# Attention units of a hybrid encoder layer in another order, and stream outputs copied in two steps

## The reference

```python
def block(i):                       # prompt, queries of 128-row block i
    s = jnp.where(mask, _mla_logits(qb, k_nope, kpe), NEG_INF)
    p = jax.nn.softmax(s, axis=-1)
    return jnp.einsum('bhqk,bkhd->bqhd', p, v)
# streams, branch A: softmax over 128 cached + 16 new latent keys
p = jax.nn.softmax(_mla_logits(q, k_nope, kpe_all), axis=-1)
# streams, branch B: the same keys, with a sink in the denominator
e = jnp.exp(s - m); p = e / (jnp.sum(e) + jnp.exp(sink - m))
o = jnp.einsum('bgjtk,bkgd->btgjd', p, v_all)
proj = jnp.einsum('btnc,ncd->btnd', stack([o_mla, o_swa]), w_branch)
```

## Time and profile before

| | |
|---|---|
| median of 3 runs | 882.08 us (881.89 to 882.47) |
| the profiled execution, its own time | 882.5 us |
| its span (first to last instruction) | 880.7 us |
| TensorE busy, share of the span | 861.0 us, 98% |
| VectorE busy | 565.5 us, 64% |
| ScalarE busy | 401.7 us, 46% |
| granted TensorE clock | 1.0 in the whole span |

### The profile page before, as it was taken

The page is one execution under the profiler, slowest core; times in us unless marked ns, Lnnn a source line. Parts: engine busy times, 40 slices in busy tenths (PEclk is TensorE's granted clock), DMA queues, the critical chain, the costliest instruction groups (busy, mean ns, idle before and its releaser), DMA issues.

```text
span 880.7 us, 13801 instructions
## 1 busy us (share of the span) xinstructions
PE 861.0 (98%) x5347; PEld 779.8 (89%) x5347; DVE 565.5 (64%) x930; ACT 401.7 (46%) x813; POOL 36.6 (4%) x56
## 2 busy tenths in 40 slices
PE   8999999999999989999999999999999999999997
PEld 7888999998667769998799999999999998888886
DVE  5548799948845775654789777777777774433224
ACT  5213464436545664434765545445444552333112
POOL 0300000060510000000000000000000000000000
PEclk9999999999999999999999999999999999999999
DMA  7513253569340004538331332223322335222203
GB/s 278 166 45 93 53 155 116 150 194 212 58 119 1 1 2 146 179 109 311 104 109 49 97 96 84 72 85 97 96 75 73 95 120 214 78 90 73 72 24 120
DMA packets 117969, 94.87 MB, mean 108 GB/s; under 512 B 25376, under 2 KB 101168, under 8 KB 117760
## 3 DMA queue, kind: packets, MB, share of 16 engines
q1 hardware_dynamic: 115744, 90.12, 33.9%
q0 software_dynamic: 896, 1.92, 0.7%
q10 hardware_dynamic: 1264, 1.94, 0.6%
HBM read 81.83 MB, written 12.40 MB: 107 GB/s over the span
## 4 chain that ended last, share of the span: by engine, by line
PE 86%; DVE 6%; ACT 5%; issue 1%; DMA 1%; DVEq 0%; POOL 0%; ACTq 0%; POOLq 0%
PE ps L1350 25%; PE ps L1351 25%; PE ps L1352 25%; PE ps L1551 2%; PE ps L1562 1%; PE ps L1600 1%; DMA raw<-in_w_out 1%; PE ps L1524 1%; PE ps L1405 1%; PE ps L1594 1%; ACT probs L1062 1%; PE ps L1646 1%; DVE sc_lo L2366 1%; DVE nm_c L2071 1%; DVE x_t L1872 1%
## 5 line engine op out<-in xcount | busy, mean ns | idle before, releaser
L1859 DVE TENSOR_TENSOR wlo<-raw,whi 128x1024 fp32r<-128x1024 f32 x43 | 52.4, 1223 | 117.1 <-ACT whi L929 109.6
L929 ACT ACTIVATE whi<-raw 128x1024 fp32r<-128x1024 f32 x43 | 45.3, 1059 | 162.6 <-PE ps L1352 160.6
L1206 ACT ACTIVATE t_hi<-wd 128x512 fp32r<-128x512 f32 x84 | 52.8, 628 | 60.2 <-DVE wd L2345 55.8
L1350 PE MATMUL ps<-sc_hi,t_lo 128*128 128x320 f32 x252 | 77.9, 309 | 1.0 <-DVE t_lo L2291 1.0
L1351 PE MATMUL ps<-sc_lo,t_hi 128*128 128x320 f32 x252 | 77.8, 309 | 0.0
L1352 PE MATMUL ps<-sc_hi,t_hi 128*128 128x320 f32 x252 | 77.8, 309 | 0.0
L1350 PE MATMUL ps<-whi,gu_lo 128*128 128x512 f32 x190 | 74.0, 390 | 0.2 <-DVE gu_lo L2415 0.2
L1352 PE MATMUL ps<-whi,gu_hi 128*128 128x512 f32 x190 | 73.9, 389 | 0.0
L1351 PE MATMUL ps<-wlo,gu_hi 128*128 128x512 f32 x190 | 73.9, 389 | 0.0
L2291 DVE TENSOR_TENSOR t_lo<-wd,t_hi 128x512 fp32r<-128x512 f32 x84 | 57.5, 685 | 2.0
L1351 PE MATMUL ps<-h_lo,b_hi 128*128 128x320 f32 x168 | 51.8, 308 | 0.0
(11 more groups left out here) (326 smaller groups left out, 2409.1 us busy)
## 6 DMA issues: line engine op xcount, KB each, us to landing
raw<-in_w_gate_up SPq DMA_DIRECT2D x44, 512.0 KB, 3.8
raw<-in_w_down SPq DMA_DIRECT2D x22, 512.0 KB, 3.6
raw<-in_w_in SPq DMA_DIRECT2D x16, 512.0 KB, 3.9
raw<-in_w_in SPq DMA_DIRECT2D x12, 480.0 KB, 5.1
gates_scratch<-g_out SPq DMA_DIRECT2D x16, 320.0 KB, 2.4
gate_r<-gates_scratch SPq DMA_DIRECT2D x8, 640.0 KB, 4.0
raw<-in_w_branch SPq DMA_DIRECT2D x8, 512.0 KB, 5.5
raw<-in_w_out SPq DMA_DIRECT2D x8, 512.0 KB, 6.3
```

The lines of the kernel that those rows point to most:

```text
L929: act.activation(whi[:, r % 2, :] if to is None else to, raw[:, r, :], ACT.Copy).then_inc(w_hi, 1)
L1206: act.activation(op_parts(kind, p)[0][:], op_source(kind, p), ACT.Copy).then_inc(op_hi_rdy, 1)
L1350: pe.matmul(out, left[1], right[0], start=first, stop=False, skip_group_check=not own_group)
L1859: dve.tensor_tensor(lo[:, place, :], raw[:, r, :], hi[:, place, :].bitcast(F32), ALU.subtract).then_inc(w_lo, 1)
```

## The change

The order of the units changes from unit 8 on. Block 1 (256 wide) is now paired with the streams' banded units, and block 2 (384 wide) with block 0 in a list written out by hand. Block 0's copies of the turned probabilities go to ScalarE, its outputs go to bank 6, which the banded outputs had before, and the four banded output copies are done in two steps of two, in rounds 19 and 20. One line (`JOBS = ...`) loses a doubled name and means the same. No instruction is added or removed, apart from copies that move from VectorE to ScalarE.

```diff
 for n in range(4):
-    UNITS += [("mla_p", 2, n), ("swa_s", n, 0)]
-for n in range(4):
-    UNITS += [("mla_p", 1, n), ("mla_p", 0, n)]
+    UNITS += [("mla_p", 1, n), ("swa_s", n, 0)]
+for a, n in ((2, 0), (2, 1), (0, 0), (2, 2), (0, 1), (2, 3), (0, 2), (0, 3)):
+    UNITS.append(("mla_p", a, n))
...
-OUT_BANK = {("mla_p", 3): 6, ("mla_p", 2): 7, ("mla_p", 1): 7, ("mla_p", 0): 1, ("swa_s", 0): 6}
+OUT_BANK = {("mla_p", 3): 6, ("mla_p", 2): 7, ("mla_p", 1): 7, ("mla_p", 0): 6, ("swa_s", 0): 6}
...
     if kind == "mla_p" and a >= 2:
         return "both"
-    return "dve" if (kind, a) == ("mla_p", 0) else "act"
+    return "act"
...
 # ScalarE
-                if 0 <= i - 4 - SWA_LAST < 4:
-                    o_part(SWA_LAST, i - 4 - SWA_LAST)
+                if 0 <= i - 4 - SWA_LAST < 2:
+                    for n in range(2 * (i - 4 - SWA_LAST), 2 * (i - 4 - SWA_LAST) + 2):
+                        o_part(SWA_LAST, n)
...
 # VectorE: the same two lines in its loop, and
             def o_part(u, n):
-                dve.wait_ge(o_hi if n == 3 else o_part_hi, GROUP[u] + 1 if n == 3 else n + 1)
+                dve.wait_ge(o_hi if n >= 2 else o_part_hi, GROUP[u] + 1 if n >= 2 else 2)
```

More of the change, by code:

```diff
@@ L80 @@
 BEHIND = [("qabs", 3), ("v", 3)]
-JOBS = TURNSJOBS = TURNSJOBS = TURNS + AHEAD + [job for chunk in CHUNK_JOBS for part in chunk for job in part] + BEHIND
+JOBS = TURNS + AHEAD + [job for chunk in CHUNK_JOBS for part in chunk for job in part] + BEHIND
 def chunk_jobs(c, part):
```

## The result

The changed kernel takes 883.25 us (median of 13 runs, 882.51 to 886.6) against 882.57 us (13 runs of before beside them, 881.89 to 883.21). The ratio is 1.0018, with a 95% interval of 1.001 to 1.0025: slower by about 1.6 us, where 0.4 us was forecast. (The ratio takes in all runs: their means are 884.11 and 882.52 us. The medians are only 0.7 us apart.) The loss is four times the forecast one. That the median lies inside the stated range of 880.7 to 884.1 us is luck, as the next lines show. The 13 times don't spread evenly: seven lie at 882.5 to 883.3 us and six at 884.9 to 886.6 us. The first seven have a mean granted TensorE clock of 0.999, the six have 0.996 or 0.997. The median is the highest of the seven; with one more run in the second group it would have been near 885.

The account below looks back on a forecast made before the run. TensorE, busy 98% of the span, was taken as the bound, so only its waits or work count. Waits removed (-4.4 us) and new waits (+4.8 us) gave +0.4 us, a median of 882.5 us, range 880.7 to 884.1.

Parts of the forecast that it names:

- The ceiling: All TensorE waits of the stage gone: eight waits costing about 4.6 us, a gain of 0.5% at most.
- the rule for a wait: TensorE is busy 98% of the span, so only a wait of TensorE, or TensorE work, can change the time.
- the price of a wait: A TensorE wait costs its idle time plus 0.14 us, because matmuls overlap.
- Part 1: Block 1 with the banded units: three of four copy waits go, 1.7 us removed.
- Part 2: Banded copies in two steps: three normalisation waits and the projection's 0.41 us go, 2.4 us removed.
- small gaps: Gaps too short for the wait view go with the waits of the banded-copy rounds, taken at 0.3 us.
- Part 3: Block 2 with block 0: waits come before turns 16, 18, 19, 20 and outputs of unit 18, 4.8 us added.
- the rule on queues: ScalarE, VectorE and GpSimdE queues are strict FIFO, so two waiting low halves hold up a row maximum on VectorE.
- The faster one: Low halves hold nobody, so round 20's row maximum starts sooner: 2.5 us less, 880.0 us; chance 0.14.
- The slower rival: Rounds 9 to 15 too short for the chain behind them: seven waits of 0.3 us, 884.6 us; chance 0.13.

Follow-up runs that it names:

- the repeat: The changed kernel timed again with no edit: 885.14 us (10 runs) against 882.42 for the kernel before, ratio 1.0025.
- the copies-alone run: Kernel before in its own order of units, only the banded outputs' copies in two steps of two: 882.16 us against 882.42, ratio 1.0002.
- the copy first: Changed kernel with ScalarE's copy of the turned unit ahead of the exponentials in rounds 17, 19, 21: 881.45 us against 882.42, ratio 0.9996.
- the low halves later: Changed kernel with VectorE's four banded low halves moved to the end of round 20: 881.95 us (11 runs) against 882.10 for the kernel before.

## Why the prediction was wrong, by its own steps

**What bounds the kernel.** The ceiling and the rule for a wait hold. The step that failed is the price of a wait: "a wait costs more than its idle time, because matmuls overlap", idle plus 0.14 us, and with it the sum made from it. That price is complete as long as the clock stays full. I put 4.8 us of waits into five rounds and never asked what TensorE's clock would do in them; all rows that I had read were at 1.0. So the sum had this term at nothing. By their times and clocks 13 of 23 runs had the stretch at half clock, at 2.7 to 2.8 us a time; the profile caught it in one of them. In the first set that is 6 / 13 x 2.7 = 1.3 us, and with the 0.3 us of the first group it makes the measured 1.6; in the repeat it is 7 / 10 x 2.8 = 2.0 us, and with 0.2 it makes the measured 2.2. The sum's own terms were nearly right.

**Part 1.** Right. The three copy waits of the banded rounds went, and no wait came in their place. A pair of these rounds takes 4.22 us, counted as 4.19.

**Part 2.** Right for the change as a whole, since none of those waits is there any more; but the two steps by themselves win nothing, which the copies-alone run shows: they bring other waits. The 0.3 us for small gaps was a guess.

**Part 3.** Each of the five waits came in its place, and four were ended by the instruction that was named. Turn 19 was not: the count has it wait for ScalarE's copy of unit 18, but the profile shows it behind VectorE's normalisation of unit 19, which ended last. From start to start they cost 313.75 - 311.81 - 0.58 = 1.36 us (1.3 in the prediction), 319.45 - 318.09 - 0.58 = 0.78 (0.8), 322.58 - 320.59 - 1.39 = 0.60 (0.4), 324.29 - 322.58 - 0.75 = 0.96 (0.6) and 326.88 - 324.66 - 0.58 = 1.64 (1.7). That is 5.3 us for 4.8. As the stage grew by 0.63 us, 4.7 us must have gone where 4.4 were counted, so that the two errors partly cancel. The two that were taken too small stand behind the low halves; the pairs of copies take 0.77 us on ScalarE and 0.85 us on VectorE in the rows of this profile. In VectorE's timeline, with ScalarE's copy of unit 18 as the last line:

```profile
320.03 0.85 DVE L2124 TENSOR_TENSOR os_lo<-ps,os_hi 64x256 fp32r<-64x256 f32 x2 [1.34 <-ACT os_hi L1088]
320.89 0.42 DVE L2072 TENSOR_REDUCE nm_c<-ps 128x2 f32<-128x256 f32 x1
...
321.55 0.96 DVE L2082 TENSOR_TENSOR probs<-probs,inv_c 128x768 f32<-128x768 f32 x1
323.27 0.87 DVE L2124 TENSOR_TENSOR os_lo<-ps,os_hi 64x256 fp32r<-64x256 f32 x2 [0.77 <-ACT os_hi L1088]
324.17 0.96 DVE L2072 TENSOR_REDUCE nm_c<-ps 128x2 f32<-128x768 f32 x1
...
322.05 0.38 ACT L1076 ACTIVATE probs_T<-ps 128x256 f32<-128x256 f32 x1
```

The normalisation ends at 322.51, the copy at 322.43, and turn 19 starts at 322.58. The row maximum of round 20 directly behind two low halves is what the rule on queues said.

**The rivals.** The faster one ended as an edit: with the low halves behind the row maximum of round 20 its five fastest runs are some 1.5 us faster than the first group (881.35 for 882.85 on average), less than the 2.5 us of the rival, because turn 20 keeps its 1.51 us. In that run the row maximum of round 21 still starts directly behind low halves, and from it to turn 20 it is 325.61 - 322.90 = 2.71 us, the same as 326.88 - 324.17 in the changed kernel: exponentials, ScalarE's copy behind them, then the turn. The slower rival, waits in the banded rounds, did not come. The case that came was none of mine.

**Open.** Why the clock falls in some executions and not in others is not settled: the rows of the two groups before the fall agree within a few hundredths, apart from a start that is shifted by 0.4 us. Several kernels, the one before among them, also have runs 0.9 to 2 us above their fastest with a clock of 0.997 or 0.998: four of eleven with the copies alone, four of eleven with the copy first, six of eleven with the low halves later. No profile of these was caught, and in the profiles at hand a mean of 0.998 or 0.999 comes from the end of the program, when TensorE has no work left (in the profile of before too the clock is at half from 880 us on). The pairing without the two steps was not tried: block 0's first outputs need bank 6 empty in round 21, which four steps to round 22 don't give.

## What to carry to other kernels

When a change gathers TensorE's waits in one place, price them twice: their idle time, and a possible stretch at half clock behind them. Look at single times, not only at the median, and set them beside the mean granted clock of each run; two groups with two clocks point to a mechanism, which a profile of each group can show. In a pipeline over four engines in fixed order, ask for each instruction that waits what stands behind it, and put the one that others wait for first; here two such moves of a copy and of four low halves turned a loss of 0.2% into a gain of 0.2%.

## What the runs showed of the hardware that was not expected

The granted clock fell to half in a wait of 1.51 us, with TensorE busy for 4.48 us of the six microseconds from 320 us on, and came back some 7 us later although TensorE was at work again from 327.27 us on. Another execution of the same kernel with the same waits and 4.49 us of busy time in the same stretch kept the full clock. With the two rounds ahead filled the clock still fell in one execution, for 3.4 us. More matmuls made the kernel faster: with 27 transposes of no use the median was 2.3 us lower than that of the unedited kernel beside it, and the mean 1.7 us.
